# Later turns of normed heads, an earlier start of a feed-forward net, and decay sums loaded ahead of weights

## What is computed

```python
# forgetting attention ("fox"), 16 heads of 64
q, k, v, z, f = split(h @ w_in)
q, k = rms_norm(q) * g_q, rms_norm(k) * g_k      # per head
# even layer of the second block: gated delta net, chunks of 64, both directions
decay = exp(where(tril, gc[i] - gc[j], -inf))     # gc: running sums of the log decay
m = where(strict, (kb @ k.T) * decay, 0)
tmat = inverse(m + eye)                           # unit lower triangular
u, w, qk = tmat @ vb, tmat @ (kb * exp(gc)), (q @ k.T) * decay
v_new = u - w @ s;  o = (q * exp(gc)) @ s + qk @ v_new;  s = s * g_last + k_dec.T @ v_new
# odd layer: neighbourhood attention beside grouped-query attention ("gq", "gkv")
q, k = rope(rms_norm(q) * q_norm), rope(rms_norm(k) * k_norm)
# behind each mixer of the second block
h = h + gate * rms_norm(swiglu(modulate(rms_norm(h)), w_gate, w_up, w_down))
```

## Time and profile before

| what | value |
|---|---|
| median of three runs | 3622.81 us (3622.74 to 3628.21) |
| profiled execution, its own time | 3621.67 us |
| its span | 3619.9 us |
| TensorE busy | 3223.1 us, 89% |
| VectorE, ScalarE, GpSimd busy | 48%, 34%, 8% |
| chain that ended last | TensorE 71%, VectorE 16%, ScalarE 6%, DMA 4% |

### The profile page before, as it was taken

The page is one execution under the profiler, slowest core; times in us unless marked ns, Lnnn a source line. Parts: engine busy times, 40 slices in busy tenths (PEclk is TensorE's granted clock), DMA queues, the critical chain, the costliest instruction groups (busy, mean ns, idle before and its releaser), DMA issues.

```text
span 3619.9 us, 55356 instructions
## 1 busy us (share of the span) xinstructions
PE 3223.1 (89%) x23642; PEld 2622.1 (72%) x23642; DVE 1742.7 (48%) x2804; ACT 1244.5 (34%) x2222; POOL 287.9 (8%) x284
## 2 busy tenths in 40 slices
PE   6988987998998897798998888999999888789998
PEld 4767766755776786678886567888887775578876
DVE  2355435345434648666674554333334346644334
ACT  3325324345431456322223444211112325642211
POOL 0020010000002000133340000000000101000000
PEclk9999998999999998899998999999999899999999
DMA  4282231281224120222111001221121214012221
GB/s 173 98 304 85 93 104 60 75 308 61 94 71 169 37 99 24 72 93 80 66 52 57 24 1 35 70 70 52 65 70 47 82 46 82 1 54 97 93 93 70
DMA packets 164111, 301.30 MB, mean 83 GB/s; under 512 B 9654, under 2 KB 30967, under 8 KB 163609
## 3 DMA queue, kind: packets, MB, share of 16 engines
q1 hardware_dynamic: 148112, 278.71, 22.7%
q10 hardware_dynamic: 13641, 11.55, 1.0%
q0 software_dynamic: 2112, 7.50, 0.8%
HBM read 289.62 MB, written 6.76 MB: 82 GB/s over the span
## 4 chain that ended last, share of the span: by engine, by line
PE 71%; DVE 16%; ACT 6%; DMA 4%; issue 1%; POOL 0%; ACTq 0%; DVEq 0%; SPq 0%; POOLq 0%
PE psum L370 17%; PE psum L372 16%; PE psum L371 16%; PE psum L2114 4%; PE psum L827 3%; PE psum L851 3%; PE psum L836 3%; PE psum L497 2%; DVE weights_r L328 2%; DMA feat<-decay_sums 1%; DVE arena L2016 1%; DVE arena L750 1%; DVE x_lat L753 1%; ACT weights_r L321 1%; DVE arena L2024 1%
## 5 line engine op out<-in xcount | busy, mean ns | idle before, releaser
L328 DVE TENSOR_TENSOR weights_r<-weights,weights_r 128x2048 fp32r<-128x2048 f32 (+3 forms) x176 | 369.2, 2119 | 564.6 <-ACT weights_r L321 564.4
L370 PE MATMUL psum<-feat_r,weights_r 128*128 128x512 f32 (+2 forms) x1544 | 554.9, 359 | 32.5 <-DVE feat_r L631 24.8
L370 PE MATMUL psum<-weights_r,feat_r 128*128 128x512 f32 (+2 forms) x1344 | 533.1, 397 | 23.5 <-DVE feat_r L631 14.9
L371 PE MATMUL psum<-feat_r,weights_r 128*128 128x512 f32 (+2 forms) x1544 | 550.5, 357 | 0.0
L372 PE MATMUL psum<-feat_r,weights_r 128*128 128x512 f32 (+2 forms) x1544 | 549.4, 356 | 0.0
L321 ACT ACTIVATE weights_r<-weights 128x2048 fp32r<-128x2048 f32 (+3 forms) x176 | 307.9, 1771 | 639.1 <-DMA weights<-in_w_ffn_gate 223.1
L371 PE MATMUL psum<-weights_r,feat_r 128*128 128x512 f32 (+2 forms) x1344 | 525.5, 391 | 0.0
L372 PE MATMUL psum<-weights_r,feat_r 128*128 128x512 f32 (+2 forms) x1344 | 525.4, 391 | 0.0
L370 PEld LDWEIGHTS psum<-feat_r,weights_r 128*128 128x128 f32 (+1 forms) x1544 | 295.4, 191 | 79.4 <-DVE feat_r L631 25.7
L371 PEld LDWEIGHTS psum<-feat_r,weights_r 128*128 128x128 f32 (+1 forms) x1544 | 295.6, 191 | 42.7
L372 PEld LDWEIGHTS psum<-feat_r,weights_r 128*128 128x128 f32 (+1 forms) x1544 | 294.7, 191 | 43.3
(11 more groups left out here) (444 smaller groups left out, 4686.0 us busy)
## 6 DMA issues: line engine op xcount, KB each, us to landing
weights<-in_w_mod SPq DMA_DIRECT2D x48, 2048.0 KB, 12.8
weights<-in_gla_w_in SPq DMA_DIRECT2D x24, 1024.0 KB, 7.3
weights<-in_w_ffn_gate SPq DMA_DIRECT2D x20, 1024.0 KB, 6.4
weights<-in_w_ffn_up SPq DMA_DIRECT2D x20, 1024.0 KB, 5.1
weights<-in_w_ffn_down SPq DMA_DIRECT2D x20, 1024.0 KB, 6.5
weights<-in_fox_w_in SPq DMA_DIRECT2D x16, 1024.0 KB, 6.7
weights<-in_sgu_w_in SPq DMA_DIRECT2D x12, 1024.0 KB, 6.2
weights<-in_gla_w_out SPq DMA_DIRECT2D x8, 1024.0 KB, 7.0
```

The source lines that it names most:

```text
L328: dve.e.tensor_tensor(WEI_r[:, s * SLOT:s * SLOT + n], WEI_t[:, s * SLOT:s * SLOT + n], WEI_r[:, s * SLOT + HALF:s * SLOT + HALF + n].bitc ...
L370: pe.e.matmul(ps, lh, rh, start=first, stop=False)
L371: pe.e.matmul(ps, lh, rl, start=False, stop=False)
```

## The change

It has six parts.

- (a) `sp_rows_first`: SP, before it loads into a slot that the gated delta net's chunk of step n has freed, also waits until the decay rows of step n + 2 have landed.
- (b) The norm at the end of feed-forward net 0 has its affine and low part three tiles behind the scaling, not two (`norm_lag`), and TensorE gets one more turn behind its loop.
- (c) Queries and keys of the forgetting attention are turned two products behind their own.
- (d) The first gate and up products of feed-forward net 0 run in three ranges of 256 tokens, so that the first needs two tiles.
- (e) `dve_gdn`: `dve_kq(n + 1, 1)` moves from before `dve_first` to behind level 5. At the start the second half of the rest moves behind `dve_first`.
- (f) In the odd layer, `gq` and `gkv` are turned two products behind.

```diff
--- before.py
+++ after.py
@@ -302,6 +302,16 @@
                 where[q0 + k] = (hi[:, k, :], lo[:, k, :] if lo is not None else None)
         return where
 
+    sides_at = [c for c, entry in enumerate(plan) if entry[0] in ("w_mod", "w_mod_2")]
+    gdn_sides_at = sides_at[len(sides_at) - 2 * SIDES_GDN:]
+
+    def sp_rows_first(sp, before):
+
+        if before in gdn_sides_at:
+            n = gdn_sides_at.index(before) // 2 * 2 + 2
+            if n < STEPS:
+                sp.wait_ge(*decay_in.of((D_, "rows", n)))
+
     def sp_weights(sp):
         for c, (name, index, k0, kt, n0, n, split) in enumerate(plan):
             if name == "w_out_odd_2" and n0:
@@ -311,6 +321,7 @@
             for j, (s, q0, q, before) in enumerate(chunks[c]):
                 if before is not None:
                     sp.wait_ge(*B.of(("weights", before)))
+                    sp_rows_first(sp, before)
                 raw = WEI_t[:, s * SLOT:s * SLOT + q * n].rearrange("p (k n) -> p k n", k=q)
                 sp.e.dma_start(raw, src[:, q0:q0 + q, :]).then_inc(*w_in[s].put(("weights", c, j)))
 
@@ -549,7 +560,12 @@
 
         order = norm_order(pre)
         early = len(order) - len(tiles)
-        return [order[j - 2 + early] if j - 2 + early >= 0 else None for j in range(len(tiles))]
+        at = early - norm_lag(pre)
+        return [order[j + at] if j + at >= 0 else None for j in range(len(tiles))]
+
+    def norm_lag(pre):
+
+        return 3 if pre == ("pre", 5) else 2
 
     turns = {}
 
@@ -1429,7 +1445,7 @@
                 done = pe.e.transpose(ps[:, m * P:(m + 1) * P], f_qn[r][:, m * P:(m + 1) * P], ident)
             done.then_inc(*B.put((T, "turned", n0, t)))
 
-        late = None
+        late = []
         for n0 in range(0, 3072, NMAX):
             if n0 == 2048:
                 pe_linear_feat(pe, (T, "f"), "fox_w_in", 4096, 16, [(0, 512)])
@@ -1442,9 +1458,10 @@
                 pe_product(pe, c, ps, [(feat_tile(k, t), where[k]) for k in range(KT)], [((T, "qkv"), n0, t)] + ends)
                 if n0 == 0:
                     pe_turn_next(pe, ("pre", 2))
-                if late is not None:
-                    turned(*late)
-                late = (n0, t) if n0 < 2048 else None
+                if len(late) == 2 or n0 >= 2048 and late:
+                    turned(*late.pop(0))
+                if n0 < 2048:
+                    late.append((n0, t))
         pe.wait_ge(*A.of((T, "in")))
         pe.wait_ge(*V.of((T, "in")))
         pe_attention(pe, T, f_units, f_att[0:3], f_att[3:5], f_out, SIDES_FOX)
@@ -1484,17 +1501,18 @@
                         act.e.activation(f_v[:, t, n0 - 2048:n0 - 2048 + NMAX], K.at[at],
                                          ACT.Copy).then_inc(*A.put(K.frees(A, at)))
                     continue
-                if late is not None:
-                    act.wait_ge(*V.of((T, "qn", *late)))
+                if late:
+                    act.wait_ge(*V.of((T, "qn", *late[-1])))
                 act_head_squares(act, K.at[at], f_sq, at, [(T, "squares", n0, t)])
                 act_head_root(act, f_ss, FDH, V.of((T, "sums", n0, t)), [(T, "root", n0, t)])
-                if late is not None:
-                    turned(*late)
-                late = (n0, t)
+                if len(late) == 2:
+                    turned(*late.pop(0))
+                late.append((n0, t))
             if n0 == 2048 - NMAX:
-                act.wait_ge(*V.of((T, "qn", *late)))
+                act.wait_ge(*V.of((T, "qn", *late[-1])))
                 act_take(act)
-                turned(*late)
+                for one in late:
+                    turned(*one)
                 gates()
         A.mark((T, "in"))
         act.wait_ge(*V.of((T, "in")))
@@ -1629,7 +1647,7 @@
 
     def ffn_ranges(n, ranges):
 
-        return [(0, 256), (256, 256)] if n == 0 and len(ranges) == 1 else ranges
+        return [(c0, 256) for c0 in range(0, sum(c for _, c in ranges), 256)] if n == 0 else ranges
 
     FFN_ORDER = [DFF // NMAX * NMAX] + list(range(0, DFF // NMAX * NMAX, NMAX))
     ffn_gates = [[COND[:, 0:NMAX], SIDE_t[:, :]], [ar(2 * h0_, NMAX), ar(2 * h0_ + NMAX, NMAX)]]
@@ -1663,6 +1681,8 @@
                 pe_product(pe, c, ps, [(hidden(k, t), where[k]) for k in range(nf // P)], [at] + ends)
             if beside[j] is not None:
                 pe_turn_next(pe, ffn_next(i))
+        if ffn_next(i):
+            pe_turn_next(pe, ffn_next(i))
 
     def act_ffn(act, i, tiles):
         T, E, pre = ("ffn", i), ("endffn", i), ffn_next(i)
@@ -1706,7 +1726,7 @@
             if pre:
                 act_norm_root(act, pre, t, V.of((E, "resid", t)))
         if pre:
-            for t in tiles[-2:]:
+            for t in tiles[-norm_lag(pre):]:
                 act_affine(act, pre, t)
             A.mark((pre, "feat"))
 
@@ -2447,10 +2467,11 @@
     def dve_gdn(dve):
         dve_gdn_begin(dve)
         dve_dif(dve, 0)
-        for which in range(2):
-            dve_kq(dve, 0, which)
-            dve_kq_rest(dve, 0, which)
+        dve_kq(dve, 0, 0)
+        dve_kq_rest(dve, 0, 0)
+        dve_kq(dve, 0, 1)
         dve_first(dve, 0)
+        dve_kq_rest(dve, 0, 1)
         for n in range(STEPS):
             more, behind = n + 1 < STEPS, n > 0
             dve_level(dve, n, 1)
@@ -2468,10 +2489,10 @@
             dve_state(dve, n)
             dve_level(dve, n, 4)
             if more:
-                dve_kq(dve, n + 1, 1)
                 dve_first(dve, n + 1)
             dve_level(dve, n, 5)
             if more:
+                dve_kq(dve, n + 1, 1)
                 dve_kq_rest(dve, n + 1, 1)
             dve_side(dve, gdn_side(n))
             dve_corner(dve, n)
@@ -2862,21 +2883,21 @@
         pe_linear_feat(pe, (W_, "nak"), "w_in_odd_2", 512, 512, both_ranges)
         for which, c0, n, tiles, src, width in (("gq", 1536, 512, LAT, w_qn, 4), ("gkv", 2048, 256, ALL, w_kn, 2)):
             c, where = pe_take(pe, "w_in_odd_2", 0, KT, c0, n)
-            late = None
-            for t in [*tiles, None]:
-                if t is not None:
+            for j in range(len(tiles) + 2):
+                if j < len(tiles):
+                    t = tiles[j]
                     at = (W_, which, t)
                     ps = K.open(pe, at)
                     names = [at, ("weights", c)] if t == tiles[-1] else [at]
                     pe_product(pe, c, ps[:, 0:n], [(feat_tile(k, t), where[k]) for k in range(KT)], names)
-                if late is not None:
+                if j >= 2:
+                    late = tiles[j - 2]
                     at = (W_, which, late, "turned")
                     ps = K.open(pe, at)
                     pe.wait_ge(*V.of((W_, which, late, "normed")))
                     for m in range(width):
                         done = pe.e.transpose(ps[:, m * P:(m + 1) * P], src[late % 2][:, m * P:(m + 1) * P], ident)
                     done.then_inc(*B.put(at))
-                late = t
         B.mark((W_, "in"))
         pe.wait_ge(*A.of((W_, "in")))
         pe.wait_ge(*V.of((W_, "in")))
@@ -2924,9 +2945,10 @@
                     act.e.activation(w_gv[:, t, :], K.at[at][:, 128:256], ACT.Copy).then_inc(*A.put())
                 act_head_squares(act, K.at[at][:, 0:n], w_sq[:, 0:n], at, [(W_, which, t, "squares")])
                 act_head_root(act, w_ss[:, 0:nh], DH, V.of((W_, which, t, "sums")), [(W_, which, t, "root")])
-                if t:
-                    turned(t - 1)
-            turned(tiles[-1])
+                if t >= 2:
+                    turned(t - 2)
+            for t in tiles[-2:]:
+                turned(t)
         A.mark((W_, "in"))
         act.wait_ge(*V.of((W_, "in")))
         before = None
```

## The result

| kernel | median, us | lowest to highest | against before, with its 95% interval |
|---|---|---|---|
| before, four runs | 3625.43 | 3622.74 to 3628.21 | 1 |
| the change, four runs | 3576.60 | 3567.51 to 3581.02 | 0.9862 (0.984 to 0.9884) |

The change is faster by 1.4%, about 49 us. Its four executions lie 13.5 us apart, more than those of before. The profiled execution of the change took 3581.02 us, the slowest of the four, with a span of 3579.2 us. Its trace is set against that of before, 3621.67 us: 40.7 us less.

What follows compares the result with a forecast made beforehand. The prediction took the chain of waits as the bound, TensorE making 71% of it, so time is won where TensorE idles or runs slowly. Its terms summed to −33.5 us against the profiled 3621.67, giving 3588 us, range 3568 to 3606.

Steps and rivals of the forecast that it cites:

- the clock: TensorE's clock may fall at eight new waits (six chunks, the net's start, the tail of fox): +8 us.
- the bank wait: Gated delta net: TensorE waits 2.1 us in each of six even steps for a bank the moved pair frees, 12.5 us.
- the step that foresaw 2.3: End of fox: VectorE's split of the next weights ends its first half later than TensorE wants it, +2.3 us.
- slow stretch: Feed-forward net 0: matmuls run slowly behind both old waits, and about one such stretch, 3.7 us, goes.
- the splits: Feed-forward net 0: each of four splits into products of 256 columns costs 0.3 us, +1.2.
- the bank wait costs nothing: Rival, gated delta net: the freed bank is another or the chunk is late anyway; 3576 us, down to 3568; chance 0.17.
- the first case: Whole kernel: the forecast itself, each part near its sum, 3580 to 3597 us; chance 0.52.
- The late rows: Rival, gated delta net: decay rows come late for another reason than the two loads, 15 us less gain, 3603; chance 0.10.
- the clock falls at all new waits: Rival: TensorE's clock falls at all eight new waits, 19 us in place of 8, 3599, up to 3605; chance 0.15.
- never through one: Slower rival, even steps: the clock stays down through the step, 20.3 us more each, 3710 for all six; chance 0.04.

Runs made afterwards that it cites:

- e3: The kernel before with only SP's wait for the decay rows ahead of its loads added: 3596.61 us, 0.9925 of before.
- e1: The change, but inside the gated delta net's steps the second key and query products stand before the first level's start again: 3562.28 us, 0.9832 of before.
- e6: The change with the old order in the gated delta net's steps, and fox's queries and keys turned one product behind, as before: 3571.67 us, 0.9859 of before.
- e7: The change with the gated delta net steps' old order and net 0's first gate and up products in ranges of 512 and 256 tokens: 3575.49 us.
- e8: The change with the gated delta net steps' old order, without net 0's late affines and the odd layer's later turns: 3573.55 us, 0.9867 of before.
- e4: The change without SP's wait for the decay rows: 3596.18 us, 0.9928 of before.

## Why the prediction was right, and where its sizes were off

Each part in us, forecast and measured (medians; "off" says how much better than forecast):

| term | forecast | measured | from | off |
|---|---|---|---|---|
| (a) | −22.4 | −25.4 | e3 | 3.0 |
| (e) and the clock | +12.4 + 8 | +14.3 − 2.2 | e1; start from the timeline | 8.3 |
| (c) | −10.4 | −9.4 | e6 | −1.0 |
| (d) | −10.4 | −13.2 | e7 | 2.8 |
| (b) and (f) | −10.7 | −11.3 | e8 | 0.6 |
| sum | −33.5 | −47.2 | | 13.7 |

The 47.2 stand against 48.8 measured at once. The direction and the range held, and so did the mechanism of each part; the number for the clock did not. Two small slips stand in the working: the terms of (c) add up to −10.5, and 33.5 below 3621.67 with the 1.1 that the median lies above it is 3589.3, where I gave 3588. The result is 48.8 us below its own before, and 45.1 below the 3621.67.

- **The term furthest off is the clock's price on top of the bank wait.** "I take a little under half of 8 × 2.4 = 19" was added to waits of 2.1 us each. The runs show 8.6 us of waiting and 5.7 beside it, which makes 14.3 where I had 12.5 + 1.2 for the banks and most of the 8 for the clock. In the trace of e4 the same six waits cost no clock to speak of. (c) and (d) were measured with the clock's loss of their own new waits in them, and (c) came out 1.0 worse than its term, (d) no worse. So some 6 to 7 of the 21.7 for banks and clock had nothing to pay for.
- **The bank wait** is 1.43 us and not 2.1. VectorE comes to level 5 sooner, since L2378, 1.5 to 1.7 us before, takes 0.68 in the new order (below).
- **(a)** was priced by step 9, 32.19 us, as an undisturbed odd step. It still had 1.4 us of VectorE's wait in it, but its neighbours are shorter in any case: the four odd steps take 30.02, 32.61, 31.38 and 32.03 us in e3, 31.5 in the mean, which makes 25.1 for four where I had 22.4. The −2.2 at the start of (e) is TensorE's wait of 8.83 us for the first level, where it was 11.08; I had costed 1.3 from the nearest pair.
- **(c)** lost 2.38 us at the tail, by the step that foresaw 2.3. The stretch behind it (711 to 716) has a granted clock of 0.66. Beside before, instruction by instruction, TensorE was 13.5 us ahead at 697 and 8.7 at 727, so the tail cost 4.8, and half of it was not in the term of (c).
- **(d)** The waits were forecast at 4.6 us and are 4.0. Place by place the part is worth 11.4 us (e7), against the 10.4 of the sum. The waits alone make 8.5 of it. No run shows the 3.7 for a slow stretch by itself; 2.9 are left for it less the splits, where the sum had 3.7 − 1.2 = 2.5. And what the medians show above that lies where the code is unchanged.
- **(b), (f)** 3.9 us at the net's end against 4.1, and 6.2 in the odd layer against 6.6.
- **The rivals.** The measured 3576.6 is all but the number of "the bank wait costs nothing" (3576), and yet that rival's mechanism is refuted by the six waits: the number came by other ways, the clock's term that was too large and (a) and (d) that were too small. It lies below the 3580 to 3597 of the first case too, whose mechanisms held: that the range took it in rests on the low end lent by the refuted rival, and that is luck. The late rows are refuted by e3. That the clock falls at all new waits is refuted by the chunk of step 4, 3.64 us behind its wait. The clock stayed low for parts of a step, never through one: the lowest mean in an even step is 0.93.

Behind the same wait of 1.43 us the chunk of step 2 took 5.34 us and that of step 4 3.64. The Trainium skill, "TensorE: Matmul & The Clock Gate", section "What's actually happening", has the throttled state as the default one, which activity releases. The first chunk agrees with that, and the second shows that this alone doesn't tell which of the waits will cost something. For the splits, a 256 column matmul starts each 0.12 us in the change too (2219.90 to 2220.02), as it did before.

## What to carry to other kernels

When a read of a PSUM bank is moved later on one engine, look up which step opens that bank next: banks that go round tie two lists of work together that share no data, and here one pair of reads moved behind one level cost some 14 us where all else won some 60. A load that nobody needs yet can hold back one that somebody waits for: one wait on the issuing queue brought the longest transfer from 13.4 us to 4.6 and paid 25 us. Undo each part of a change by itself: here the change got 14 us faster when one of its parts was taken back.

## What the runs showed of the hardware

The scalar_tensor_tensor of `dve_first` (128x512) takes 0.68 us or 1.6 us, by its place in the list. In e1, in even steps:

```profile
L2398 DVE SCALAR_TENSOR_TENSOR weights<-feat,const x6: 1526/1614/1714, 1536.1 to 1850.6; 128x512 f32<-128x512 f32 x6
```

In the change, six times at less than half of it:

```profile
L2398 DVE SCALAR_TENSOR_TENSOR weights<-feat,const x6: 683/684/684, 1535.9 to 1864.3; 128x512 f32<-128x512 f32 x6
```

In before, where it is slow, one of GpSimd's operations of 1.26 us (L2499) began at 1615.87, beside it. In the change GpSimd's operation (L2520) began at 1602.42, when it had ended, and the pair L2389 took 2.39 us beside the next one, against 1.71 for the same pair in before. The records fit two engines that slow each other down, but no run took GpSimd's work away, so this stays a reading.
